# Latent products of a two-layer block: load order, ScalarE and VectorE order, and a shared key projected in four row groups

## What is computed

```python
cq = _rmsnorm(b_cq, gq)                      # 384 latent columns of x @ w_in
ckv = _rmsnorm(b_ckv, gkv)                   # 256 latent columns of x @ w_in
qh = _split_heads(cq @ w_uq, MLA_HEADS)      # 8 heads, 64 plain + 32 rotated
q_b = jnp.concatenate([qh[..., :MLA_NOPE], _rope(qh[..., MLA_NOPE:], pos)], axis=-1)
kvh = _split_heads(ckv @ w_ukv, MLA_HEADS)
k_rope = _rope(b_kr[:, None], pos)           # ONE key of 32 columns, shared by all heads
k_b = jnp.concatenate([kvh[..., :MLA_NOPE],
                       jnp.broadcast_to(k_rope, (B, MLA_HEADS, S, MLA_ROPE))], axis=-1)
yb = mla_attention(q_b, k_b, kvh[..., MLA_NOPE:])
yb = _merge_heads(yb) * jax.nn.silu(b_z)
```

## Time and profile before

| what | value |
|---|---|
| median of 3 runs | 2122.8 us (2121.53 to 2125.31) |
| profiled execution, its own time | 2122.98 us |
| its span in the trace | 2121.2 us |
| TensorE busy | 2082.5 us, 98% |
| VectorE, ScalarE, GpSimd busy | 1398.6, 1298.9, 676.4 us |
| mean granted TensorE clock | 0.993 of full speed |

### The profile page before, as it was taken

How to read it: one execution, slowest core, us unless ns; L and a number is a source line. 1 busy time by engine, 2 the same in 40 slices (tenths; PEclk the granted TensorE clock), 3 DMA queues, 4 the chain that set the end, 5 groups by cost and what they waited for, 6 DMA issues and landing times.

```text
span 2121.2 us, 33729 instructions
## 1 busy us (share of the span) xinstructions
PE 2082.5 (98%) x13391; PEld 1868.4 (88%) x13395; DVE 1398.6 (66%) x1428; ACT 1298.9 (61%) x1452; POOL 676.4 (32%) x335
## 2 busy tenths in 40 slices
PE   9989999998999999999999999999999999999998
PEld 8979999988999898999998888888888888888887
DVE  1544323344413794323787999999999999999997
ACT  4556545455644544444545777777777777777776
POOL 5646885845788303988201000000000000000000
PEclk9989999999999999999999999999999999999999
DMA  7434554633455434666447999999999999999995
GB/s 245 132 104 139 179 197 152 194 97 118 160 198 180 124 117 140 200 198 192 145 140 246 385 374 334 375 357 370 358 351 365 356 374 350 363 354 373 367 365 205
DMA packets 308658, 529.07 MB, mean 249 GB/s; under 512 B 13890, under 2 KB 153314, under 8 KB 308544
## 3 DMA queue, kind: packets, MB, share of 16 engines
q1 hardware_dynamic: 307520, 525.92, 71.3%
q0 software_dynamic: 736, 1.00, 0.2%
q10 hardware_dynamic: 288, 0.52, 0.1%
HBM read 525.84 MB, written 1.05 MB: 248 GB/s over the span
## 4 chain that ended last, share of the span: by engine, by line
PE 89%; ACT 3%; DVE 3%; POOL 2%; DMA 1%; issue 1%; SPq 0%; ACTq 0%; DVEq 0%; POOLq 0%
PE bank L776 87%; POOL weights_low L3234 2%; PE bank L1641 1%; ACT sc L1786 1%; ACT weights_high L1789 1%; DVE sc L2497 1%; DMA ring<-in_w_in_dram 0%; PE bank L1037 0%; DVE cq L2497 0%; DMA ring<-in_mla_w_uq_dram 0%; DMA ring<-in_w_ple_dram 0%; DVE nmax L2524 0%; DVE sc L2489 0%; DVE h L2497 0%; PE bank L787 0%
## 5 line engine op out<-in xcount | busy, mean ns | idle before, releaser
L2489 DVE TENSOR_TENSOR expert_weights_low<-ring_experts,expert_weights_high 128x2048 fp32r<-128x2048 f32 x336 | 764.8, 2289 | 72.5 <-ACT expert_weights_high L1789 72.4
L1789 ACT ACTIVATE expert_weights_high<-ring_experts 128x2048 fp32r<-128x2048 f32 x336 | 647.4, 1927 | 165.7 <-PE bank L776 161.4
L3234 POOL TENSOR_TENSOR weights_low<-ring,weights_high 128x1024 fp32r<-128x1024 f32 x252 | 616.8, 2470 | 280.4 <-ACT weights_high L1789 168.9
L1789 ACT ACTIVATE weights_high<-ring 128x1024 fp32r<-128x1024 f32 x294 | 304.0, 1057 | 327.7 <-PE bank L776 288.0
L776 PE MATMUL bank<-x_high,weights_high 128*128 128x256 f32 x1024 | 230.1, 281 | 5.0 <-POOL weights_low L3234 4.8
L776 PE MATMUL bank<-x_high,weights_low 128*128 128x256 f32 x1024 | 226.8, 278 | 0.0
L776 PEld LDWEIGHTS bank<-x_high,weights_high 128*128 128x128 f32 x1024 | 184.2, 189 | 7.9 <-issue 6.4
L776 PEld LDWEIGHTS bank<-x_high,weights_low 128*128 128x128 f32 x1024 | 184.1, 189 | 0.5 <-issue 0.5
L776 PE MATMUL bank<-expert_weights_high,gathered_high 128*128 128x512 f32 x456 | 180.7, 396 | 0.3 <-DVE gathered_low L2497 0.3
L776 PE MATMUL bank<-expert_weights_high,gathered_low 128*128 128x512 f32 x456 | 177.8, 390 | 0.0
L776 PE MATMUL bank<-expert_weights_high,gathered_high_b 128*128 128x512 f32 x448 | 177.5, 396 | 0.0
(11 more groups left out here) (380 smaller groups left out, 3780.3 us busy)
## 6 DMA issues: line engine op xcount, KB each, us to landing
ring_experts<-in_moe_w_gate_dram SPq DMA_DIRECT2D x112, 1024.0 KB, 7.0
ring_experts<-in_moe_w_up_dram SPq DMA_DIRECT2D x112, 1024.0 KB, 6.8
ring_experts<-in_moe_w_down_dram SPq DMA_DIRECT2D x112, 1024.0 KB, 6.5
ring<-in_w_in_dram SPq DMA_DIRECT2D x62, 1024.0 KB, 5.3
ring<-in_w_merge_dram SPq DMA_DIRECT2D x24, 1024.0 KB, 5.1
ring<-in_w_out_dram SPq DMA_DIRECT2D x14, 1024.0 KB, 5.2
ring<-in_ffn_w_gate_dram SPq DMA_DIRECT2D x11, 1024.0 KB, 5.3
ring<-in_ffn_w_up_dram SPq DMA_DIRECT2D x11, 1024.0 KB, 5.4
```

What stands on the lines that cost most here:

```text
L1789: return nc.scalar.activation(dst, src, ACT.Copy, scale=scale)
L2489: return nc.vector.tensor_tensor(dst, x, z, op)
L3234: nc.gpsimd.tensor_tensor(half_of(wlo[:, q_slot, :], t, width), half_of(ring[:, slot, :], t, width), half_of(whi[:, q_slot, :], t, width). ...
```

## The change

The units are loaded in another order. ScalarE copies the first latent unit before it splits `az0`, the second and third after the key's copy, and does the exponentials of softmax 3 after the drains of the queries, with `after("mc1")` ahead of them. VectorE does the key's rotation and the first values between the two halves of softmax 3. GpSimd does the first latent low part right after `mc1`'s low part. TensorE's order stays, but the shared key's eight products go in turn to four groups of 32 output rows, so that each group holds the sum of two; all 128 rows are copied to `kr`, and `r4`'s constant now has the unit matrix four times below each other too, so that the spreading product adds the four.

```diff
-    c[0:ROPE, C_REP:C_REP + P] = np.tile(np.eye(ROPE, dtype=np.float32), P // ROPE)
+    c[:, C_REP:C_REP + P] = np.tile(np.eye(ROPE, dtype=np.float32), (P // ROPE, P // ROPE))
...
-    + [("w_in", 2048, 256, 8), ("w_in", 2304, 256, 8), ("w_in", 2560, 128, 8), ("w_in", 2688, 32, 8), ("w_in", 1536, 256, 8)]
-    + [("w_uq", c, 384, 3) for c in (0, 384)] + [("w_ukv", c, 512, 2) for c in (0, 512)]
+    + [("w_in", 2048, 256, 8), ("w_in", 2304, 256, 8), ("w_uq", 0, 384, 3), ("w_in", 1536, 256, 8)]
+    + [("w_in", 2560, 128, 8), ("w_in", 2688, 32, 8), ("w_uq", 384, 384, 3)] + [("w_ukv", c, 512, 2) for c in (0, 512)]
...
                         for kk in range(8):
-                            ins = mm(views(b)[0:ROPE, 1, :], w[:, kk, :], xT[:, kk, :], kk == 0, kk == 7)
+                            r0 = ROPE * (kk % 4)
+                            ins = mm(views(b)[r0:r0 + ROPE, 1, :], w[:, kk, :], xT[:, kk, :], kk < 4, kk >= 4)
...
-                        mm(views(b)[:, 0, :], cst[0:ROPE, C_REP:C_REP + P], kr[0:ROPE, :], True, True).then_inc(full.h, 1)
+                        mm(views(b)[:, 0, :], cst[:, C_REP:C_REP + P], kr[:, :], True, True).then_inc(full.h, 1)
...
                 take_y(1)
+                latent_high(0)
                 after("mc0")
...
-                copy(kr[0:ROPE, :], views(b)[0:ROPE, 1, :]).then_inc(dr_a.h, 1)
-                latent_high(0)
-                latent_high(1)
+                copy(kr[:, :], views(b)[:, 1, :]).then_inc(dr_a.h, 1)
                 take_turned(2)
...
                 copy(kr[:, :], views(b)[:, 0, :]).then_inc(dr_a.h, 1)
+                latent_high(1)
+                latent_high(2)
                 gate_tanh("az0", 0)
-                latent_high(2)
                 take_y(2)
                 latent_high(3)
-                exps(3)
+                after("mc1")
                 for j in range(2):
                     drain(layer, f"un{j}", qb[:, 2 * j:2 * j + 2, :], MLA_D ** -0.5)
                     b = G1.wait_full(act, layer, f"ur{j}")
                     act.mul(qb[:, 4 + j, :], views(b)[:, 0, :], MLA_D ** -0.5).then_inc(dr_a.h, 1)
+                exps(3)
                 for j in range(2):
                     drain(layer, f"kn{j}", kb[:, 2 * j:2 * j + 2, :])
 
-                after("mc1")
                 after("az0")
...
+                    if between:
+                        between()
                     dve.wait_ge(p_exp.h, p_exp.at(layer, n + 1))
...
-                softmax(3)
-                rope("rk", kr[:, :].unsqueeze(1), 0).then_inc(roped.h, 1)
-                values(0)
+                def key_and_values():
+                    rope("rk", kr[:, :].unsqueeze(1), 0).then_inc(roped.h, 1)
+                    values(0)
+
+                softmax(3, key_and_values)
...
-                    if q == SPLIT1.index("az0"):
-                        for i in range(LATENT1):
+                    if SPLIT1.index("mc1") <= q <= SPLIT1.index("az0"):
+                        for i in range(1) if q == SPLIT1.index("mc1") else range(1, LATENT1):
```

More of the change, by code:

```diff
@@ L218 @@
 UNITS1 = [PLE_UNITS + REST1, REST1[:1] + PLE_UNITS + REST1[1:]]
-TAKEN1 = [list(range(len(UNITS1[0]))), [1, 2, 0] + list(range(3, len(UNITS1[1])))]
+LATER1 = [("w_in", 1536, 256, 8), ("w_uq", 0, 384, 3)]
+USED1 = [x for x in PLE_UNITS + REST1 if x not in LATER1]
+_at = USED1.index(("w_uq", 384, 384, 3))
+USED1[_at:_at] = LATER1
+TAKEN1 = [[units.index(x) for x in USED1] for units in UNITS1]
 N_UNITS1 = len(UNITS1[0])
@@ L2510, in drain, with softmax @@
                     nc.vector.tensor_copy(dst, views(b)).then_inc(dr_v.h, 1)
-                def softmax(n):
+                def softmax(n, between=None):
                     kind, bb = BATCHES[n]
```

## The result

The changed kernel took **2092.06 us** (median of 4 runs, 2092.01 to 2092.87), the kernel before 2122.16 us beside it (2121.03 to 2125.31): a ratio of 0.9857, 95% interval 0.984 to 0.9874. The forecast was 2092.3 us. The profiled execution took 2092.87 us, with a span of 2090.9 us, 30.3 us shorter than before.

What follows compares the result with a forecast made beforehand. TensorE, busy 98%, was taken as the bound, its waits costing twice through a lower clock. Gains of 16.18 and 14.71 us, less 0.4, made 30.5 us: 2092.3 us; range 2088 to 2096 (0.60), ends 2086 and 2103.

Steps and rivals of the forecast that it cites:

- Steps 1 and 2: Up to `B 2`: earlier loads and latent copy, plus the key's four groups, start `B 2` 1.66 us sooner per layer.
- Step 2, `r4`: Spreading product of the shared key: 128 rows for 32 have the same number of columns and cost the same (0).
- step 1: Loads and latent weights: `exps(2)` waits only for its maxima and comes 1.66 us sooner in each layer.
- Step 3: Second half of `w_uq` loaded sooner: waits of 0.86 and 1.87 us go (layer 1: 1.75 and 1.87).
- Steps 4 and 5: `exps(3)` behind the queries' drains, `az1`'s weights sooner: waits of 3.90 and 2.27 us go (layer 1: 5.32, 2.28).
- step 4: Before `rk`: `exps(3)` behind the drains, `un0` drained 2.8 us before TensorE asks; 3.90 us go (layer 1: 5.32).
- rival (b): ScalarE stands in `after("mc1")` longer than reckoned, TensorE loses up to 3 us a layer: 2095 to 2102; chance 0.10.
- Step 6: VectorE's rope and values between softmax 3's halves: some 2 us per GpSimd collision, 0.2 us a layer allowed.
- Step 7: Granted clock on TensorE: without the stops, stretches run at 1.00, gaining 5.62 us in layer 0, 1.83 in layer 1.
- Rival (a): The clock falls anyway, after TensorE's wait of about 1 us before `B 2`: 2094 to 2098; chance 0.15.

Runs made afterwards that it cites:

- e2: The kernel before, with only the shared key's four groups added: 2126.0 us, ratio 1.0005.
- e1: The changed kernel with the shared key projected in one group of 32 rows again, all orders staying changed: 2095.59 us, ratio 0.9865.
- e3: The changed kernel with the exponentials of softmax 3 put back ahead of the drains of the queries: 2101.97 us, ratio 0.9892.
- e7: The kernel before with only ScalarE's order changed: `after("mc1")` ahead of the queries' drains, `exps(3)` behind them: 2123.4 us, ratio 1.0003.
- e9: The changed kernel with ScalarE's and VectorE's order around softmax 3 as before; loads, latent copies and key stay changed: 2108.34 us, ratio 0.9937.
- e10: The kernel of e5 with the first half of `az0`'s products in front of the transposes of batch 2: 2091.89 us, ratio 0.986.
- e5: The changed kernel with the key's two SBUF operations moved after softmax 3, only the bank-draining product staying between the halves: 2090.61 us, ratio 0.9852.
- e6: The changed kernel with `latent_high(1)` back in its old place on ScalarE, ahead of `take_turned(2)`: 2092.76 us, ratio 0.9858.
- e12: The changed kernel word for word, timed again: 2092.0 us, ratio 0.986.
- e8: The kernel before with ScalarE's order and VectorE's order around softmax 3 changed; loads, latent copies and key as before: 2106.57 us, ratio 0.9929.

## Why the prediction was right

The layers' gains, from the stretches and stops above (forecast in brackets; layer 0, then layer 1):

- *Reading*: the first of the five stops, 0.28 us before `B 2`, ended with VectorE, and not with ScalarE or GpSimd as the others did; the sum does not use it.
- *Steps 1 and 2*, up to `B 2`: 1.60 and 1.75 us (1.66 each): 2.56 us of products less the larger stop (in layer 1 before, 11.65 us of waiting less the four of the earlier trace rows leave 0.43). Right in mechanism and size, and as said what is late next is softmax 2 and not TensorE. e2 shows that without step 1 the key's groups give nothing, e1 that without them 3.5 us are missing, of which 0.8 us are the next point.
- *Step 2, `r4`*: 0.38 and 0.38 us (0). The term "cost the same (0)" was mis-sized.
- *Step 3*: 2.73 and 3.62 us (the same). No wait of ScalarE for `w_uq` is left.
- *Steps 4 and 5*: 6.17 and 7.60 us (the same). e3, e7 and e9 bring these waits back or take them away at the named places. Mis-sized was the cover of step 4, 2.8 us. I had counted GpSimd's work at its undisturbed 2.92 us; beside VectorE's latents it takes 121.39 + 2.04 - 119.40 = 4.0 us, and `az1`'s load comes that much later: `un0` is drained at 131.34, not 130.0. And TensorE asks for the bank at 131.63, 1.2 us sooner than the forecast's 132.79. 0.3 us are left, enough here, but e10 used them up: rival (b) was nearer than the 0.10 said.
- *Step 6*: -0.73 and -0.73 us (-0.2 each). Rotation and softmax 3 met collisions, as the step's own worst case had it: it said near 145, and the second half ends at 141.58 + 3.23 = 144.81. The stop is there because TensorE was at `B 3` at 144.14 and not at 145.5.
- *Step 7*, the clock: what is left of each layer's gain, 6.96 and 3.05 us (5.62 and 1.83). Most of it is the granted clock. In the kernel before, 8.04 us from 130.55 ran at 0.79, 6.01 us from 142.48 at 0.51 and 7.15 us from 154.56 at 0.76, which makes 1.69 + 2.94 + 1.72 = 6.35 us; in layer 1 5.54 us from 485.62 ran at 0.63, 2.05 us. The forecast had less because it left out `rk` itself (142.48 to 143.11) and set layer 1's rows against layer 0's, though layer 1's products follow each other more slowly at the full clock (0.118 us apart for 0.113). What the other 0.6 and 1.0 us are stays open. The mechanism is the forecast's: a mean clock of 0.89 and 0.94 became 1.00. Rival (a) did not happen: in the layers of the profiled execution the stops of 1.24 us did not lower the clock, nor did they in e5, e6 and e12.

That is 17.11 and 15.67 us where the forecast had 16.18 and 14.71 (less 0.4). The sum still came out at 2092, because 2.5 us were lost outside the two stretches, in places that the forecast took as unchanged: a slower pace of the products at full clock, and the start and end of the program. So the agreement to 0.2 us is partly luck; the layers by themselves were 2.3 us better than forecast. Whether the runs without a profile lost the same is open: on record is only their mean clock, 0.998 against 0.997 in the profiled one, with times 0.8 us shorter.

## What to carry to other kernels

A change of order can be worth nothing in parts and a lot as a set. Two parts were run alone, and each moved a wait to the next engine in line: the groups alone and ScalarE's order alone measured 1.0005 and 1.0003. The two halves of the change, e8 and e9, whose parts belong together, gave 15.4 and 13.3 us, and these simply add. VectorE's order alone and the load order alone were not run. So before a part is costed, ask which instruction stands next behind the bank or the load that it frees, on every engine, and whether two-operand SBUF work of VectorE will then lie beside a GpSimd pass. And keep a number for the spare time of each hidden chain: here the load of `az1` is hidden by 0.3 us, and e10 was the change that did not fit into them.

## What the runs showed of the hardware that was not expected

- Two VectorE operations that take 1.15 us undisturbed took 5.20 to 5.38 us beside GpSimd's passes; a cast with one SBUF operand took 1.42 us for 0.43; GpSimd's pass over the second `w_uq` half took 4.0 us beside VectorE's latents, where that over the first half, of the same size, takes 2.92.
- Eight products with 32 output rows and 128 input rows took 3.6 us in one group of rows and 1.0 us in four (e1 and the changed kernel, `mc2` less its eight full products).
- One product with 32 input rows between full ones cost 0.38 us more than the same with 128 rows (0.62 us to the next product in e1, 0.24 in the changed kernel).
- The clock fell in stretches in which the profile has TensorE busy without a break, in the kernel before and after (0.74 at 725 to 738 us; 0.83 at 1000 to 1010 us), each time at the 32 products with 8 columns, in 22 of 28 such places. It did not fall in the layers behind stops of 1.24 us, nor in e10 behind 1.67 us; it did in e2 behind 2.85 us and in e3 behind 3.92 us.
- At a granted clock of 1.00 the same 24 products took 2.72 us in one execution and 2.83 us in the other, over stretches of 10 to 30 us (1009 to 1029 us of the changed kernel is one).
